# Norm weights folded into the weight tiles, and a norm whose halves are transposed and evicted in four pieces

## The reference

```python
def _rms_norm(x, g):
    y = x * lax.rsqrt(jnp.mean(x * x, -1, keepdims=True) + NORM_EPS)
    return y * g

for l in range(2):                                    # first block
    x = x + 0.5 * swiglu(_rms_norm(x, norm_ffn1[l]), gate1[l], up1[l], down1[l])    # d_ff 2816
    h = _rms_norm(x, norm_mix[l]) @ w_in[l]                                         # 1024 -> 2944
    mix = concat(rwkv7(h[:, :1280]), dilated_attention(h[:, 1280:2432]), conv(h[:, 2432:]))
    x = x + mix @ w_out[l]
    x = x + 0.5 * swiglu(_rms_norm(x, norm_ffn2[l]), gate2[l], up2[l], down2[l])
# swiglu(h) = (silu(h @ gate) * (h @ up)) @ down
# second block: input projection, MoBA attention, convolution and pooling, output projection,
# layer norm, a feed-forward with a 3-tap convolution, layer norm. It has no RMS norm weights ahead of a product.
```

## Time and profile before

| | us |
|---|---|
| median of 3 runs | 1485.84 |
| the profiled execution | 1481.22 |
| its span, first to last instruction | 1479.4 |
| PE busy in it | 1400.2 (95%) |
| PEld busy | 1227.6 (83%) |
| DVE busy | 942.7 (64%) |
| ACT busy | 717.7 (49%) |
| POOL busy | 182.1 (12%) |

### The profile page before, as it was taken

One profiled execution on the slowest core, in us unless ns is written; L12 is line 12 of the kernel. 1 busy time (PEld: TensorE's weight loads), 2 busy tenths in 40 slices (PEclk: granted clock), 3 DMA queues, 4 the chain that ended last, 5 costly groups with the idle time before them and its releaser, 6 DMA issues.

```text
span 1479.4 us, 25137 instructions
## 1 busy us (share of the span) xinstructions
PE 1400.2 (95%) x10017; PEld 1227.6 (83%) x10017; DVE 942.7 (64%) x1246; ACT 717.7 (49%) x1010; POOL 182.1 (12%) x177
## 2 busy tenths in 40 slices
PE   6999999998999999999999999899999998799995
PEld 5888889977788887888879988688888897799994
DVE  5666576675665656665566675665665666576676
ACT  6444466353654445544456544554444544344442
POOL 3000000297000000000000089100000042000000
PEclk9999999998999999999999999899999999899998
DMA  9655364200775544755446210556554833455520
GB/s 334 228 176 193 104 221 126 83 2 2 230 237 186 193 130 156 262 184 190 133 138 203 67 59 2 173 200 198 172 169 150 278 115 114 143 173 199 196 85 29
DMA packets 172340, 230.58 MB, mean 156 GB/s; under 512 B 4639, under 2 KB 153799, under 8 KB 172005
## 3 DMA queue, kind: packets, MB, share of 16 engines
q1 hardware_dynamic: 169664, 222.71, 45.8%
q10 hardware_dynamic: 1989, 6.63, 1.2%
q0 software_dynamic: 608, 0.12, 0.0%
HBM read 228.38 MB, written 2.63 MB: 156 GB/s over the span
## 4 chain that ended last, share of the span: by engine, by line
PE 80%; POOL 10%; DVE 6%; ACT 2%; issue 1%; DMA 1%; ACTq 0%; SPq 0%; DVEq 0%; POOLq 0%
PE bank L466 44%; PE bank L563 22%; PE bank L564 11%; POOL mix L1694 5%; POOL proj L1692 5%; DVE hT L785 1%; DVE up_lo L451 1%; DMA w_gate<-in_ffn_w_gate_dram 1%; PE bank L1000 1%; PE bank L1043 0%; DVE x L720 0%; DVE work L2100 0%; ACT hT L777 0%; DVE x L2000 0%; DVE x L2006 0%
## 5 line engine op out<-in xcount | busy, mean ns | idle before, releaser
L563 PE MATMUL bank<-hT,gate_hi 128*128 128x512 f32 x704 | 255.2, 404 | 6.1 <-DVE hT L785 6.1
L563 PE MATMUL bank<-hT,up_hi 128*128 128x512 f32 x704 | 250.6, 399 | 4.0 <-DVE up_lo L451 4.0
L451 DVE TENSOR_TENSOR down_lo<-w_down,down_hi 128x2048 fp32r<-128x2048 f32 x67 | 153.4, 2290 | 96.3 <-ACT down_hi L446 96.3
L643 ACT ACTIVATE work<-bank 128x256 f32<-128x256 f32 x176 | 67.3, 385 | 285.5 <-PE bank L564 285.5
L564 PE MATMUL bank<-hT,gate_lo 128*128 128x256 f32 x704 | 199.6, 284 | 0.0
L564 PE MATMUL bank<-hT,up_lo 128*128 128x256 f32 x704 | 197.5, 281 | 0.0
L451 DVE TENSOR_TENSOR gate_lo<-w_gate,gate_hi 128x2048 fp32r<-128x2048 f32 x67 | 153.8, 2296 | 63.9 <-ACT gate_hi L446 63.9
L451 DVE TENSOR_TENSOR up_lo<-w_up,up_hi 128x2048 fp32r<-128x2048 f32 x72 | 162.5, 2257 | 31.6 <-ACT up_hi L446 31.6
L446 ACT ACTIVATE down_hi<-w_down 128x2048 fp32r<-128x2048 f32 x67 | 128.4, 1917 | 105.8 <-PE bank L466 105.8
L563 PEld LDWEIGHTS bank<-hT,gate_hi 128*128 128x128 f32 x704 | 134.8, 191 | 40.7 <-issue 7.8
L563 PEld LDWEIGHTS bank<-hT,up_hi 128*128 128x128 f32 x704 | 132.2, 188 | 37.9 <-DVE up_lo L451 5.3
(11 more groups left out here) (322 smaller groups left out, 2406.5 us busy)
## 6 DMA issues: line engine op xcount, KB each, us to landing
w_gate<-in_ffn_w_gate_dram SPq DMA_DIRECT2D x44, 1024.0 KB, 5.3
w_up<-in_ffn_w_up_dram SPq DMA_DIRECT2D x44, 1024.0 KB, 5.3
w_down<-in_ffn_w_down_dram SPq DMA_DIRECT2D x44, 1024.0 KB, 5.1
w_up<-in_w_in_dram SPq DMA_DIRECT2D x12, 1024.0 KB, 8.8
w_down<-in_w_in_dram SPq DMA_DIRECT2D x11, 1024.0 KB, 5.5
w_gate<-in_w_up_dram SPq DMA_DIRECT2D x11, 1024.0 KB, 5.8
w_up<-in_w_up_dram SPq DMA_DIRECT2D x11, 1024.0 KB, 5.1
w_down<-in_w_down_dram SPq DMA_DIRECT2D x11, 1024.0 KB, 5.0
```

Of the source, the lines that this page charges most:

```text
L451: dve.tensor_tensor(staged[kind][1][:, 0:cols], slot[sl][:, 0:cols], staged[kind][0][:, 0:cols].bitcast(F32), ALU.subtract).then_inc(split ...
L563: pe.matmul(bank[:, :], w[0][:, c, at], hpair[:, :, c, :], start=c == 0, stop=False)
L643: act.activation(low[:, q, j * SEQ:(j + 1) * SEQ], psum[2 * q + j][:, SEQ:], ACT.Copy)\
```

## The change

1. `act_high` and `dve_low` take a norm weight (`gain`). With one, the single 128x2048 instruction becomes 8 of 128x256 (128x128 for the half tile), one for each chunk c, with the norm weight of that chunk as a per-partition column: on ACT `activation(Copy, scale=column)`, on DVE `scalar_tensor_tensor` (weight x column - high). This holds for `gate` and `up` tiles of the four feed-forward blocks of the first block and for the 12 `w_in` tiles of each mixer. `down` and `w_out` tiles and the second block keep one instruction.
2. The transposed activations carry no weight now: `act_turned` and `dve_turned` are 4 instructions of 128x512 each. `dve_norm` multiplies each row in two halves and signals each, `pe_turn` waits for each half.
3. The first 128 output columns after a norm run as 24 matmuls of 256 columns: 16 that need only the high halves of the activations (`high_ready`), then 8 with the low halves. ACT and DVE read that bank's first half alone.
4. All norm weights are loaded and transposed once at the start (`gains`, 3 DMAs on ACT's queue in place of one; two of GpSimd's row loads go), and each layer's pick, transpose and copy is gone. ACT's first split waits for `gains_ready`; in the mixer's seam its wait for `params_ready` stands behind `act_turned`.

```diff
-            act.activation(staged[kind][0][:, 0:cols], slot[sl][:, 0:cols], ACT.Copy).then_inc(high[sl], 1)
+            if gain is None:
+                ins = act.activation(staged[kind][0][:, 0:cols], slot[sl][:, 0:cols], ACT.Copy)
+            else:
+                n = cols // KC
+                for c in range(KC):
+                    at = slice(c * n, (c + 1) * n)
+                    ins = act.activation(staged[kind][0][:, at], slot[sl][:, at], ACT.Copy,
+                                         scale=gains[:, gain + c:gain + c + 1])
+            ins.then_inc(high[sl], 1)
...
+                for c in range(KC):
+                    at = slice(c * n, (c + 1) * n)
+                    ins = dve.scalar_tensor_tensor(staged[kind][1][:, at], slot[sl][:, at],
+                                                   gains[:, gain + c:gain + c + 1],
+                                                   staged[kind][0][:, at].bitcast(F32), ALU.mult, ALU.subtract)
+            ins.then_inc(split[sl], 1)
...
+                        if opening:
+                            for c in range(KC):
+                                high_ready(pe, n_norm, c)
+                                pe.matmul(bank[:, 0:SEQ], w[1][:, c, at], hT[0][:, c, :], start=c == 0, stop=False)
+                                pe.matmul(bank[:, 0:SEQ], w[0][:, c, at], hT[0][:, c, :], start=False, stop=False)
+                            for c in range(KC):
+                                h_ready(pe, n_norm, c)
+                                mm = pe.matmul(bank[:, 0:SEQ], w[0][:, c, at], hT[1][:, c, :], start=False,
+                                               stop=c == KC - 1)
...
-            dve.tensor_scalar(hN[:, t, :], x[:, t, :], rstd[:, 6 + t:7 + t], None, ALU.mult)\
-               .then_inc(S["normed"], 1)
+            for h in range(2):
+                at = slice(h * 512, (h + 1) * 512)
+                dve.tensor_scalar(hN[:, t, at], x[:, t, at], rstd[:, 6 + t:7 + t], None, ALU.mult)\
+                   .then_inc(S["normed"], 1)
...
-            for t, c, step in turned_parts(gain):
-                if c % 4 == 0:
-                    act.wait_ge(S["turned"], 4 * n + 2 * t + c // 4 + 1 + past["turned"])
-                act.activation(hT[0][:, c:c + step, t * P:(t + 1) * P], turned_bank(t, c, step), ACT.Copy,
-                               scale=col(gain, c) if gain else 1.0).then_inc(S["h_high"], 1)
+            for i, (t, c) in enumerate(PARTS):
+                act.wait_ge(S["turned"], 4 * n + i + 1 + past["turned"])
+                act.activation(hT[0][:, c:c + 4, t * P:(t + 1) * P], turned_bank(t, c), ACT.Copy)\
+                   .then_inc(S["h_high"], 1)
```

More of the change, by code:

```diff
@@ L440, in build, with gain_of, act_high @@
             FILLS.append(count)
-        def act_high(act, uses, sl, more=0, more_kind=0, kind=None, cols=2048):
+        def gain_of(uses, n):
+            return uses.layer * 24 + n * 8
+        def act_high(act, uses, sl, more=0, more_kind=0, kind=None, cols=2048, gain=None):
             kind = kind or sl[:-1]
@@ L543, in final, with pe_ffn @@
             return isinstance(g, int) and g == GROUPS - 1
-        def pe_ffn(pe, uses, f, n_norm, last="gate", gained=True, halves=True):
+        def pe_ffn(pe, uses, f, n_norm, last="gate", halves=True):
             b = f * GROUPS
@@ L558, in wide @@
                         bank = psum[2 * q + j]
[L559 to L562, removed]
+                        at = slice(j * P, (j + 1) * P)
+                        opening = isinstance(g, int) and g == 0 and name == "gate" and j == 0
+                        if opening:
[7 more added lines that the diff above has]
+                                               stop=c == KC - 1)
+                        for c in range(KC if not opening else 0):
                             pe.matmul(bank[:, :], w[0][:, c, at], hpair[:, :, c, :], start=c == 0, stop=False)
@@ L649, in group @@
                 if not final(g):
-                    act_high(act, uses, f"gate{1 - par_}", more + par_, g + 1)
+                    act_high(act, uses, f"gate{1 - par_}", more + par_, g + 1, gain=gain)
                 low_half(g, 1, 0)
@@ L688, in sum_half @@
                 at = slice(j * SEQ, (j + 1) * SEQ)
-                dve.tensor_tensor(whole[:, q, at], psum[2 * q + j][:, 0:SEQ], low[:, q, at], ALU.add)\
-                   .then_inc(S["summed"], 1)
+                if isinstance(g, int) and (g, q, j) == (0, 0, 0):
+                    dve.tensor_scalar(whole[:, q, at], low[:, q, at], 1.0, None, ALU.mult).then_inc(S["summed"], 1)
+                else:
+                    dve.tensor_tensor(whole[:, q, at], psum[2 * q + j][:, 0:SEQ], low[:, q, at], ALU.add)\
+                       .then_inc(S["summed"], 1)
             def group(g, par_, more):
@@ L697, in group @@
                 if not final(g):
-                    dve_low(dve, uses, f"gate{1 - par_}", more + par_)
+                    dve_low(dve, uses, f"gate{1 - par_}", more + par_, gain=gain)
                 sum_half(g, 1, 0)
@@ L1028, in pe_tile @@
             w = [t_[:, 0:KC * width].rearrange("p (c n) -> p c n", n=width) for t_ in staged[tile_kind(n)]]
+            if n == 0 and 0 in parts:
+                for c in range(KC):
+                    high_ready(pe, n_norm, c)
+                    pe.matmul(psum[0][:, 0:SEQ], w[1][:, c, 0:P], hT[0][:, c, :], start=c == 0, stop=False)
+                    pe.matmul(psum[0][:, 0:SEQ], w[0][:, c, 0:P], hT[0][:, c, :], start=False, stop=False)
+                for c in range(KC):
+                    h_ready(pe, n_norm, c)
+                    pe.matmul(psum[0][:, 0:SEQ], w[0][:, c, 0:P], hT[1][:, c, :], start=False, stop=c == KC - 1)
             for i in parts:
@@ L2285, in _ @@
             pe.transpose(psum[0][0:32, 256:256 + NH2], tab[0:NH2, 32:64], ident[0:NH2, 0:NH2]).then_inc(tab_psum, 1)
+            pe.wait_ge(gain_in, 48)
+            for l in range(DEPTH):
+                mm = pe.transpose(psum[3][:, 24 * l:24 * l + 24], rows[0:24, l, :], ident[0:24, 0:24])
+            mm.then_inc(gains_psum, 1)
             for l in range(DEPTH):
```

163 lines of the change are left out of this document (83 added, 80 removed).

## The result

The changed kernel took 1499.13 us (median of 4 runs, 1498.38 to 1502.32) against 1484.64 for the kernel before beside it: ratio 1.0101, 95% interval 1.0085 to 1.0117. It is slower by 15 us. The span of the profiled execution went from 1479.4 to 1497.4 us, +18.0.

A forecast was written before the change was run, and what follows sets the result against it. PE, busy 95%, bounds the kernel, so only its few waits count. Block starts 9.4, seams 3.55 and mixers 3.6 sum to +16.5 us; from the 1485.8 median the forecast is 1502, range 1487 to 1512.

The forecast's parts named there:

- Rival 1: Weight splits and openings: pieces overlap, splits hardly grow, five openings keep 1.5 us each; 1479.3 us, chance 0.13.
- Part 2: Openings, first matmul after a norm: 1.5 us sooner, 2.1 after R, the reciprocal of token tile 1.
- b: Seam to the mixer of layer 0: down_lo of tile 1 comes late, +1.6 us.
- e: Seam to the mixer of layer 1, PE slow at its start: -1.5 + 1.8 = +0.3 us.
- f: Seam to the second feed-forward block of layer 1, PE slow there: -1.5 + 2.05 = +0.55 us.
- d: Seam to the first feed-forward block of layer 1: +1.85 + 0.15 = +2.0 us.
- c: Seam to the second feed-forward block of layer 0, PE slow at its start: -1.5 + 0.3 = -1.2 us.
- Part 3: Seams: residual adds queue behind longer splits, so the norm comes later; all seams +3.55 us, bounds -7.5 to +10.
- Rival 2: Seams: residuals are not delayed because ACT's idle time covers it; total +7.3 us, 1493, chance 0.15.
- Part 4: Mixers: GpSimd's chain starts 1.4 us later, the lora product waits 0.4 more; two mixers +3.6 us.
- Rival 3: Block starts: matmuls after the new stalls run at 1.2 GHz, 1.7 us each; +6.8, 1509 us, chance 0.17.
- seam a: Program start: the first split waits for the transposed norm weights and takes longer, +0.3 us.

The follow-up runs named there:

- e2: The changed kernel with eight pieces per split but no column operand, norm weights left out of the computation: 1480.00 us, ratio 0.9981.
- e5: e3 with DVE splitting up_lo of group 1 before group 0's hidden product in each gated feed-forward block: 1480.02 us, ratio 0.9969.
- e12: e11 with each split in two overlapping halves, DVE starting on the first while ACT makes the second: 1475.74 us, ratio 0.9946.
- e1: The changed kernel with single-instruction weight splits, norm weights left out of the computation: 1469.59 us, ratio 0.9908.
- e3: The changed kernel with ACT signalling each of the eight pieces and DVE starting on each as it comes: 1487.37 us, ratio 1.0024.
- e8: The changed kernel with single-instruction splits, the norm weights entering DVE's norm multiply as a row on all partitions: 1479.05 us, ratio 0.9958.
- e11: e9 with DVE splitting up_lo of group 1 before the hidden product in a block's first group: 1481.09 us, ratio 0.9981.
- e6: e5 with, in the mixer, the sigmoid ahead of the last tile's split and lora activations ahead of tile 3's split: 1483.38 us, ratio 0.9992.
- e9: e8 with both of e6's moves in the mixer: 1478.62 us, ratio 0.9969.

## Why the prediction was right

**Part 1, the pitch of the pieces.** Right: 3.30 and 3.28 us predicted, 3.30 and 3.26 measured. Three instructions of the kernel before with the same operands gave it. Rival 1 needed a split that grows by less than 0.7 us in all; it grew by 1.4 and 1.0, and in e2, without the column operand, by 0.65 and 0.48, at a ratio of 0.998.

**The block starts.** Right, +9.4 against +9.7. e5 and e12 show the same chain from the other side: shorten it by overlap, and 12.4 us become 12.0 and 11.7.

**Part 2.** Right in place: R + 2.1 predicted, R + 2.17 to 2.18 measured at b, e and f, R + 2.28 at d and R + 2.47 at c. That the following `up` tile of a feed-forward block comes no sooner than R + 9.3 was predicted too: PE started it at R + 9.7 at c, 9.5 at d and 9.4 at f. Before, that was R + 10.8, 9.2 and 11.4: the gain was kept where PE ran slow (c and f) and not at d, as the prediction has it.

**Part 3, R moves.** Right in mechanism: +1.85 predicted at b, +1.81 measured: from the first `down` matmul of the block to R it took 164.17 us before and 165.98 after. At d it is +1.70, at e +1.77. In e1, with single splits, it is 164.30, in e3, with overlapped pieces, 165.12. Rival 2 falls with it. At f the size was wrong: from the table's mark of the output projection to R it took 18.43 us before and 19.37 after, +0.94 and not +2.05. There the first three residual adds ran 0.6 to 0.8 us apart (969.70 to 971.10) where they had stood 1.36 apart, and caught up half of the delay.

**Part 4.** +1.8 a mixer; +2.6 in layer 0: the eight half-width pieces took 2.44 us as estimated (2.4), and GpSimd began 2.1 us later relative to the mixer's tile 1: these 1.4 and a lora wait of 0.7 in place of 0.4. In layer 1 the stretch to the next block came out at -0.3 instead of +2.35, in two parts. Up to the same mark of the output projection it is +0.7 instead of +1.8: the half-clock stretch of 6.8 us stood behind PE's wait for GpSimd before (from 928.7, wait 4.3 us up to 929.4), and stands ahead of that wait now (from 929.7, wait 0.6 up to 947.6), where slow matmuls only shorten the wait. From there it is -1.0 instead of +0.55: 1.1 less at R (part 3), and the stretch behind the opening is 3.4 us in place of 6.8.

**The clock** was the step that the sum left out. Rival 3 gave it a chance of 0.17 at +6.8 us. Its mechanism did happen: behind three of four block starts the `up` tile took 1.6, 1.6 and 1.5 us longer, +4.7 together. Counted from that tile's end, the rest of the block with seam b and with seam d grew by 1.9 and 2.1 us, against 1.6 and 2.0 predicted, so those terms were sized right. But clock stretches elsewhere went: seam a came out 1.7 below the prediction, the rest of a block with seam e 1.0 below, layer 1's mixer with f 2.65 below. So it is in part luck that the sum (+16.5) lies 1.5 us from the span's growth (+18.0): +4.7 that it did not have against -5.4 at these three, which all hold a clock stretch that went, moved or shrank. In e1, half-clock time fell by 24 us, and its gain was twice the expected one. What decides where such a stretch falls the runs do not show; the fourth block start had waits of 1.3 and 1.7 us and none behind it. That stays open.

By medians the change is +14.5, less than by spans, since the profiled execution of the kernel before (1481.22) lay 3.4 under its median. The forecast of 1502 was 3 us above the 1499.13 measured.

## What to carry to other kernels

- Fold a per-channel factor where one instruction still does the tile. As a row in a multiply that exists (e8) it cost 0.26 us for each of four multiplies a norm, and 2.1 us at the program's start; as a per-partition column it cut each weight tile in eight, +1.4 and +1.0 us a tile.
- Engines that are busy 49 and 64% hid longer instructions nearly everywhere, and paid at the few places without a buffer in between: the first groups of a block and the seams. Price a change there, with the latency of the chain (both engines' terms added), not with busy time.
- A high-then-low chain of two engines gained from being cut in two halves that overlap: 0.07 and 0.09 us more work a tile instead of 1.0 and 1.4, and PE's wait at a block start fell from 1.0 to 0.2 us. Look first at what else stands ahead of the chain, such as the table load and the silu of e11's rows.

## What the hardware showed that was not expected

**VectorE and GpSimd take turns.** DVE pieces with two SBUF operands took 1.06 to 1.33 us each beside a running GpSimd (e6) and 0.35 without it, one for each GpSimd instruction; operations on a PSUM bank were not slowed (`TENSOR_REDUCE` of 128x384 took 0.55 us in both). The number of pieces sets the price: at the same place, with GpSimd running, the one instruction of e9 took 1.34 us, the two halves of e12 2.70, the eight pieces of e6 9.14.

```profile
282.14 2.70 DVE L468 TENSOR_TENSOR up_lo<-w_up,up_hi 128x512 fp32r<-128x512 f32 x2 [0.31 <-ACT up_hi L454]
```

It works the other way round too: in the kernel after, one DVE split of 2.29 us stretched the GpSimd instruction beside it to 3.04, where the five before it take 0.97 to 1.10.

```profile
349.12 2.29 DVE L466 TENSOR_TENSOR down_lo<-w_down,down_hi 128x2048 fp32r<-128x2048 f32 x1 [0.31 <-ACT down_hi L453]
```

```profile
349.20 3.04 POOL L1741 TENSOR_TENSOR proj<-proj,par 128x464 f32<-128x464 f32 x1
```

The Trainium skill, "SBUF — State Buffer", section "SBUF: two separate sides", has the rule: the pair of ports that the two share is an exclusive lock, held for a whole instruction, and a VectorE operation with two SBUF inputs takes it against a GpSimd operation that reads SBUF. The trace agrees, and adds the price: the split was held up once for each of its pieces.
